# Moving a mixture-of-experts kernel's overflow tiles ahead of its last pair of experts

## The reference: what is computed

```
t = modulate(rms_norm(x))                        # 512 tokens
g = top-1 of 4 groups;  e = top-2 of its 8 experts
hid = silu(t @ w1[e]) * (t @ w3[e])              # 1024 -> 256
out = sum over the two experts of weight * (hid @ w2[e])
x = x + gate * out
```

## Time and profile before

| | us |
|---|---|
| median of 3 runs | 1247.36 (1244.38 to 1254.65) |
| the profiled execution's own time | 1244.05 |
| its span, first to last instruction | 1242.2 |
| PE busy | 1071.7 (86%) |
| DVE busy | 620.3 (50%) |
| ACT busy | 330.4 (27%) |
| POOL busy | 94.2 (8%) |
| q1, SP's transfers | 291.39 MB, 57.9% of 16 engines' span |

### The profile page before, as it was taken

How to read it: one execution, slowest core, us unless ns; L and a number is a source line. 1 busy time by engine, 2 the same in 40 slices (tenths; PEclk the granted TensorE clock), 3 DMA queues, 4 the chain that set the end, 5 groups by cost and what they waited for, 6 DMA issues and landing times.

```text
span 1242.2 us, 15651 instructions
## 1 busy us (share of the span) xinstructions
PE 1071.7 (86%) x5804; PEld 653.8 (53%) x5804; DVE 620.3 (50%) x1500; ACT 330.4 (27%) x913; POOL 94.2 (8%) x121
## 2 busy tenths in 40 slices
PE   2799999898999999877769899898998899877775
PEld 2344444555458666544436555554458666544442
DVE  6999699786337222221146477775237222212133
ACT  3411111675220211111124455564111211111010
POOL 1000000000000011101100000000000111111111
PEclk9999999998998999999999999999998999999998
DMA  9877777207725899999977200103325899999981
GB/s 376 330 287 313 304 301 288 85 2 297 295 96 215 344 420 419 419 420 419 416 276 294 114 1 35 68 1 161 128 86 236 326 420 421 419 420 418 420 361 73
DMA packets 63042, 333.03 MB, mean 268 GB/s; under 512 B 10543, under 2 KB 10799, under 8 KB 31600
## 3 DMA queue, kind: packets, MB, share of 16 engines
q1 hardware_dynamic: 46928, 291.39, 57.9%
q0 software_dynamic: 13824, 33.37, 7.0%
q10 hardware_dynamic: 2208, 7.18, 1.5%
HBM read 316.67 MB, written 32.52 MB: 281 GB/s over the span
## 4 chain that ended last, share of the span: by engine, by line
PE 50%; DMA 23%; DVE 17%; issue 4%; ACT 4%; SPq 1%; DVEq 0%; ACTq 0%; POOLq 0%
PE PP L622 9%; PE PP L695 8%; DMA RQK<-in_moe_w 8%; DMA AHS<-in_moe_w 8%; PE PP L710 5%; DMA ring<-in_moe_w 5%; PE PP L513 4%; DVE AHS L1251 3%; PE PP L785 3%; PE PP L537 3%; PE PP L827 2%; DVE ring L1251 2%; PE PP L831 2%; PE PP L574 2%; PE PP L585 2%
## 5 line engine op out<-in xcount | busy, mean ns | idle before, releaser
L513 PE MATMUL PP<-ring,AHS 128*128 128x512 f32 x384 | 169.2, 597 | 7.2 <-DMA ring<-in_da_w_qkv 7.2
L1572 DVE TENSOR_TENSOR PS<-PS,PP 128x256 f32<-128x256 f32 x33 | 13.9, 421 | 230.6 <-PE PP L695 230.6
L513 PEld LDWEIGHTS PP<-ring,AHS 128*128 128x128 f32 x384 | 72.3, 192 | 92.1 <-issue 92.1
L622 PE MATMUL PP<-ring,AHS 128*128 128x512 f32 x256 | 113.2, 601 | 0.8 <-ACT AHS L1122 0.8
L1582 DVE SCALAR_TENSOR_TENSOR PS<-PP,small,GF 128x512 f32<-128x512 f32 x66 | 46.5, 746 | 118.8 <-PE PP L710 118.8
L695 PE MATMUL PP<-RQK,RV 128*64 128x256 f32 x768 | 86.8, 381 | 20.6 <-issue 17.0
L695 PE MATMUL PP<-ring,RV 128*64 128x256 f32 (+1 forms) x672 | 79.2, 380 | 11.5 <-issue 11.5
L695 PEld LDWEIGHTS PP<-RQK,RV 128*64 128x64 f32 x768 | 64.7, 137 | 45.7 <-issue 30.7
L695 PE MATMUL PP<-AHS,RV 128*64 128x256 f32 x640 | 72.5, 380 | 11.2 <-issue 11.2
L622 PEld LDWEIGHTS PP<-ring,AHS 128*128 128x128 f32 x256 | 49.0, 194 | 60.0 <-issue 60.0
L695 PEld LDWEIGHTS PP<-ring,RV 128*64 128x64 f32 (+1 forms) x672 | 60.4, 140 | 33.8 <-issue 20.5
(11 more groups left out here) (302 smaller groups left out, 1598.9 us busy)
## 6 DMA issues: line engine op xcount, KB each, us to landing
RQK<-in_moe_w SPq DMA_DIRECT2D x72, 1024.0 KB
ring<-in_moe_w SPq DMA_DIRECT2D x63, 1024.0 KB, 22.2
AHS<-in_moe_w SPq DMA_DIRECT2D x60, 1024.0 KB, 28.3
ring<-in_ada_t SPq DMA_DIRECT2D x24, 1024.0 KB, 22.2
AHS<-in_ada_t SPq DMA_DIRECT2D x24, 1024.0 KB, 18.6
ring<-in_da_w_qkv SPq DMA_DIRECT2D x12, 1024.0 KB, 7.0
y_d<-GF POOLq DMA_DIRECT2D x2, 4096.0 KB, 31.0
AHS<-y_d ACTq DMA_DIRECT2D x6, 1024.0 KB, 11.5
```

The source lines that it names most:

```text
L513: last = mm(PB[n % 4][:, :], HT[:, c, t * P:(t + 1) * P], us[c // 4][:, (c % 4) * NH:(c % 4 + 1) * NH], start=c == 0, stop=c == C - 1)
L622: last = mm(PB[2 * t + n][:, :], (OT, OTM)[l][:, k, t * P:(t + 1) * P], us[k // 2][:, (k % 2) * D + n * NH:(k % 2) * D + (n + 1) * NH], st ...
```

## The change

Pairs 0 to 14 run as before. Then come the branches and the overflow tiles, and then pair 15 (`BETWEEN = LAST`). An overflow tile's rows are scattered to `y_d` by POOL, so its 0/1 matrix, its four mixes and its adds go away. All overflow tiles now use the ring bank, and their loads stand on SP's queue ahead of pair 15's. The steps of a tile no longer share the pairs' semaphores but have their own (`oturn`, `omod`, `oab`, `osil`, `ohid`, `ohT`, `oy`, `oyD`), and within a tile w1 and w3 are one group of matmuls with one signal. The pairs' semaphores (`a`, `b`, `sil`, `hid`, `ht`, `hT`, `y`, `xA`, `xD`, `xgt`, `yD`) count on from layer 0 to layer 1. `load_rows` also waits for POOL's `rows`. The turn of tile 16's rows between the products of pair 15 is gone; an overflow tile turns its own. In layer 1 each token tile's mix of pair 15 is added and then at once its sum. The diff, cut to its core:

```diff
+BETWEEN = LAST
@@ sync
-                for n in range(PAIRS):
+                for n in range(BETWEEN):
                     experts(l, n)
                 sp.wait_ge(sem("ctl"), l + 1)
                 tails = sp.value_load(CTL[0:1, 0:1], min_val=0, max_val=TAILS)
                 def overflow(i, b):
...
+                        if isinstance(i, int):
+                            sp.wait_ge(sem(pair_done), PAIRS * l + BETWEEN - 1)
+                        else:
+                            sp.wait_ge(sem(f"{tile_done}{l}"), j - 1)
+                        sp.dma_start(stored(l, RING_BANK)(2 * m + b),
...
                 overflow_steps(sp, tails, overflow)
+                for n in range(BETWEEN, PAIRS):
+                    experts(l, n)
@@ tensor
+            def overflow_tile(l, i, b):
+                j, tiles = 2 * i + b, ((0, OVER, b),)
+                w = stored(l, RING_BANK)
+                pe.wait_ge(sem(f"gath{l}0"), 16 * (PAIRS // 2 + 1 + j))
+                turn_rows(0, sem(f"oturn{l}"))
+                pe.wait_ge(sem(f"wt{l}{b}"), 48 * i + 48)
+                pe.wait_ge(sem(f"omod{l}"), 2 * j + 2)
+                into_hidden(PB[2], 0, w, 0, tiles)
+                into_hidden(PB[3], 0, w, 1, tiles).then_inc(sem(f"oab{l}"), 1)
+                pe.wait_ge(sem(f"ohid{l}"), j + 1)
+                turn_hidden(sem(f"oturn{l}"))
+                pe.wait_ge(sem(f"ohT{l}"), j + 1)
+                out_of_hidden(w, tiles).then_inc(sem(f"oy{l}"), 1)
+                pe.wait_ge(sem(f"oyD{l}"), j + 1)
 
             def experts(l):
+                turn_pair(l, 0)
+                for n in range(BETWEEN):
+                    expert_step(l, n)
+                pe.wait_ge(sem("xA"), PAIRS * l + BETWEEN + 1)
+                pe.wait_ge(sem("xD"), PAIRS * l + BETWEEN + 1)
+                pe.wait_ge(sem("yD"), PAIRS * l + BETWEEN)
+                pe.wait_ge(sem(f"gath{l}0"), 16 * (PAIRS // 2 + 1))
                 pe.wait_ge(sem("ctl"), l + 1)
                 tails = pe.value_load(CTL[0:1, 0:1], min_val=0, max_val=TAILS)
                 def overflow(i, b):
...
+                    overflow_tile(l, i, b)
                 overflow_steps(pe, tails, overflow)
+                for n in range(BETWEEN, PAIRS):
+                    expert_step(l, n)
+                for t in range(T if l else 0):
+                    mix_last(1, t)
@@ scalar, load_rows
+                act.wait_ge(sem("rows"), l + 1)
@@ scalar, between the overflow tiles and pair 15
+                fn(sd[:, 7:8], eps, ACT.Silu)
@@ vector
+                for t in range(T if l else 0):
+                    add_last(1, t)
+                    add_sums(t).then_inc(sem("res"), 1)
@@ gpsimd, after pairs 0 to 14
+                def overflow(i, b):
...
+                    if b or not isinstance(i, int):
+                        pool.wait_ge(sem(f"oturn{l}"), 2 * j - 1)
+                        gather(0, token_at)
+                    pool.wait_ge(sem(f"oyD{l}"), j + 1)
+                    scatter(0, row_at)
+                    pool.wait_ge(sem(f"scat{l}0"), 16 * (half + 1 + j))
+                overflow_steps(pool, tails, overflow)
+                pool.sem_inc(sem("rows"), 1)
```

More of the change, by code:

```diff
@@ L671, in route, with turn_rows @@
                 keep_busy(3, 20)
[L673 to L677 removed]
+            def turn_rows(b, done):
                 for c in range(C):
                     last = nc.tensor.transpose(PB[c % 2][:, (c // 2) * P:(c // 2 + 1) * P], xg[b][:, c * P:(c + 1) * P], ident[:, :])
[L680 to L700 removed]
@@ new lines, in turn_rows, with turn_pair, into_hidden @@
+                last.then_inc(done, 1)
+            def turn_pair(l, n):
+                b, m = n % 2, PAIRS * l + n
+                pe.wait_ge(sem(f"gath{l}{b}"), 16 * (n // 2 + 1))
+                wait(pe, sem("xA"), m)
+                wait(pe, sem("xD"), m)
+                turn_rows(b, sem("xgt"))
+            def into_hidden(o, b, w, m, tiles):
+                for c in range(C):
+                    for s0, s1, e in tiles:
+                        last = mm(o[s0:s1, 0:FF], xgT[b][:, c, s0:s1], w(2 * m + e)[:, c * FF:(c + 1) * FF],
+                                  start=c == 0, stop=c == C - 1)
+                return last
@@ L701, in expert_step, with turn_hidden, out_of_hidden @@
+            def turn_hidden(done):
                 for c in range(2):
                     last = nc.tensor.transpose(PB[4][:, c * P:(c + 1) * P], hid[:, c, :], ident[:, :])
-                last.then_inc(sem(f"ht{l}"), 1)
-                arrived(2)
-                pe.wait_ge(sem(f"hT{l}"), n + 1)
-                wait(pe, sem(f"yD{l}"), n)
+                last.then_inc(done, 1)
+            def out_of_hidden(w, tiles):
                 for m in range(2):
@@ L710, in expert_step, with arrived @@
                             last = mm(PB[5 + m][s0:s1, :], hidT[:, c, s0:s1],
-                                      units(4 + e)[:, c * D + m * NH:c * D + (m + 1) * NH], start=c == 0, stop=c == 1)
-                last.then_inc(sem(f"y{l}"), 1)
+                                      w(4 + e)[:, c * D + m * NH:c * D + (m + 1) * NH], start=c == 0, stop=c == 1)
+                return last
+            def expert_step(l, n):
+                tiles = ((0, CAP, 0), (CAP, 2 * CAP, 1))
+                b, m, w = n % 2, PAIRS * l + n, stored(l, n)
+                def arrived(k):
+                    for e in range(2):
+                        slot, value = arrival[l][("moe", n, 2 * k + e)]
+                        pe.wait_ge(s_w[slot], value)
+                arrived(0)
+                pe.wait_ge(sem("xA"), m + 1)
+                pe.wait_ge(sem("xD"), m + 1)
+                wait(pe, sem("sil"), m)
+                into_hidden(PB[2], b, w, 0, tiles).then_inc(sem("a"), 1)
+                arrived(1)
+                wait(pe, sem("hid"), m)
+                into_hidden(PB[3], b, w, 1, tiles).then_inc(sem("b"), 1)
+                if n < LAST:
+                    turn_pair(l, n + 1)
+                pe.wait_ge(sem("hid"), m + 1)
+                wait(pe, sem("hT"), m)
+                turn_hidden(sem("ht"))
+                arrived(2)
+                pe.wait_ge(sem("hT"), m + 1)
+                wait(pe, sem("yD"), m)
+                out_of_hidden(w, tiles).then_inc(sem("y"), 1)
+            def overflow_tile(l, i, b):
[12 more added lines that the diff above has]
+                pe.wait_ge(sem(f"oyD{l}"), j + 1)
             def mix(hot, b, t, banks):
@@ L1153, in gate, with modulate_rows @@
                 fn(v, v, ACT.Exp).then_inc(sem("ele"), 1)
-            def modulate_rows(l, b, n, before):
-                act.wait_ge(sem(f"xt{l}"), n + 1)
-                wait(act, sem(f"b{l}"), before)
+            def modulate_rows(l, b, done):
                 for c in range(0, C, 2):
@@ L1556, in gate, with modulate_rows @@
                 v.tensor_copy(CTL[:, :], tailf[0:1, :]).then_inc(sem("ctl"), 1)
-            def modulate_rows(l, b, n, before):
-                dve.wait_ge(sem(f"xt{l}"), n + 1)
-                wait(dve, sem(f"b{l}"), before)
+            def modulate_rows(l, b, done):
                 for c in range(1, C, 2):
@@ L1892, in layer, with gather @@
                        allow_small_or_imprecise_dtypes=True).then_inc(sem("iota"), 1)
[L1894 to L1904 removed]
+                def gather(b, at):
                     settle()
```

261 lines of the change are left out of this document (118 added, 143 removed).

## The result

| | before | after |
|---|---|---|
| median of 20 runs each | 1246.49 (1240.26 to 1254.65) | 1254.47 (1250.82 to 1261.51) |
| ratio, with its 95% interval | | 1.0068 (1.005 to 1.0087) |
| the profiled execution's own time | 1244.05 | 1252.87 |
| its span | 1242.2 | 1251.1 |
| mean granted clock | 0.982 | 0.974 |

The forecast was 1252.5 us, worked out on the profiled execution (which took 1252.87), and "within 1%"; both hold, and the loss is clear of the noise.

What follows compares the result with a forecast made beforehand. Serial chains were taken to bound it: layer 1's end on PE and DVE, and layer 0's pair 15 through the `y_d` loads to the next weights. Layer 0 +8.6 and layer 1 +0.1, +8.7 on 1244.05, gave 1252.5 us; range 1241 to 1262.

Steps and rivals of the forecast that it cites:

- Layer 0, the jump: PE's branch over all tiles, now ahead of pair 15, stalls 6.45 us, with +0.1 to the first matmul.
- the turn's -0.3: Layer 0, pair 15: tile 16's turn leaves it while DVE's product still stands there, saving 0.3 us.
- All of it passed on by the chain: Layer 0: pair 15's delay, +7.1 us, goes in full through the `y_d` loads to the next layer's first weights.
- jumps in what is fetched are free: Rival, both layers: PE's jumps land in instructions already fetched and cost nothing, giving 1241 us; chance 0.17.
- Layer 0, the clock: Layer 0, behind the jump: PE's matmuls run slow after standing 8.8 us, +1.5 us, between 0 and 3.7.
- The rival of the full queues: Both layers: the jump's fetch waits behind streaming weights on the same DMA engines, giving 1264 us; chance 0.15.
- its extra 6.45: Layer 0: weights in flight hold the jump as much again, so that it costs 12.9 us.
- Layer 1, up to pair 15's start: Layer 1, pair 14's rows to pair 15: load, turn, modulation, products, clock +1.7 and jump +3.4 us, ending at 1209.0.
- Tile's weights: Layer 1: the tile's last load lands between 1189.4 and 1196.5, needed at 1189.8; taken as 0, bound 6.7 us.
- The end: Layer 1, adds and sums behind pair 15: done at 1237.3 against 1237.16 before, +0.1 us; outputs stay 5.0 us behind.
- bound by POOL's sum rather than by DVE: Sign expected at layer 1's end: the last add waits for POOL's sum of 2.48 us behind the fourth `y_d` load.
- up to 1 less: Layer 1's outputs: 5.0 us behind the last sum, possibly less by up to 1 us because they come spaced out.

Runs made afterwards that it cites:

- e2: The kernel before with PE's two loop copies of an overflow tile left out of its program; ratio to before 0.999 (0.9965 to 1.0015).
- e1: The changed kernel with PE's two loop copies of an overflow tile left out of its program; ratio to before 0.9984 (0.9961 to 1.0008).
- e3: The changed kernel with PE's waits for pair 14's rows, turned rows and gather moved from ahead of the count's load into the tile's code; ratio to before 0.9992.
- e5: The changed kernel with one tile copy in line and one in the loop on every engine, plus e3's moved waits; ratio to before 0.9966.
- e10: The changed kernel with 36 dummy matmuls (144 instructions) at PE's start, shifting all later PE code; ratio to before 1.0033.
- e9: e5 with dummy matmuls in the tile's gaps (14 and 7) and without PE's wait for the tile's rows at its end; ratio to before 0.9937.
- e6: e3 with 36 dummy matmuls on PE in layer 0 ahead of the load of the count; ratio to before 1.0029.

## Why the prediction was right, step by step

The prediction's sum has a slip: 1244.05 + 8.7 is 1252.75, not 1252.5. Its "+0.4%" sets that against the median of before, which is 3.3 us above the execution it adds to; like for like the sum is +0.7%, and 0.68% was measured.

The numbers are those of the profiled executions, from the start of pair 14's w2 product. The difference of the spans, 8.9 us, is made of: 2.3 less upstream (1.7 of it a product of pair 13 that ran at the low clock in before's execution, the rest not traced; I take it for chance, as e2's execution, in the old order, has that start at 616.21), 7.5 from pair 14 of layer 0 to the mla projection (41.66 less 34.14), 1.5 from there to pair 14 of layer 1, and 2.1 from there to the end (63.3 against 61.2).

How the loss divides over the stages is less sure than the total, for before's execution is only one. e2 has the old order, short jumps and the time of before (0.999), yet from pair 14's w2 product to the mla projection it took 37.15 us and not 34.14:

```profile
653.36 7.61 PE L788 MATMUL PP<-ring,AHS 128*128 128x384 f32 x16 [6.10 <-DMA ring<-in_mla_w_in]
```

Against e2 the changed kernel loses 4.5 us in that stretch, gains 1.1 in the next and loses 2.9 at the end; with 0.6 upstream that makes the 6.9 by which the spans differ. Before starts pair 14's w2 product 2.9 us later than e2, and both reach the mla projection at the same time (653.23 and 653.36). So read the stage figures below, which are against before, as good to 2 or 3 us.

- **Layer 0, the jump: right.** Predicted 7.4 us to pair 15's start (the turn's -0.3 lies behind it), measured 7.44. The jump was 5.93 (taken 6.45), the load of the count and what lies around it 0.5 more than taken. e1 shows that 5.6 of it is the jump, e3 that the waits ahead of it uncover it. How much of it arrives is less sure: pair 15's w2 product comes 7.1 us later than in before (23.48 against 16.40) and 5.6 later than in e2 (17.88), where pair 15's second product stood 2.05 us for its weights and ran at half rate. "All of it passed on by the chain" holds against before's execution, not against e2's. That jumps in what is fetched are free was right as a mechanism (e1, e5, e10's layer 1) and wrong for this kernel, as its chance of 0.17 said.
- **Layer 0, the clock: right in size, not in its account.** Predicted +1.5. Pair 15's two products lost 2.1 us by it (9.48 against 7.34), but I had missed a saving: before, the second product waited 1.24 us for its weights (the gap that the profile calls "issue"; with the delay the weights are there, and the 64 run in one). The mla projection's first 16 matmuls took 6.79 us for 5.40, which is most of the 1.5 behind it; but in e2 they took 7.61, so this isn't the change's doing. The sum of layer 0 and the stretch to layer 1 is 9.0, predicted 8.6; against e2 it is 3.4. That the two agree so well is in part luck.
- **The rival of the full queues did not come.** The jump took 5.93 us with weights in flight, no longer than 6.45. Layer 0's is longer than layer 1's in every kernel that has both (5.93, 6.09, 6.25, 4.93, 5.15 against 3.33, 3.63, 3.73, 3.87, 3.68), and the q8 packet shows where: it begins 3.4 us behind the branch in layer 0 and 1.0 in layer 1, while the packet itself (1.1 and 0.9 us) and the rest behind it (1.4) are alike. What holds it back was not tried; only the transfers in flight differ that I know of (281 GB/s at 624 to 626 us, 13 at 1213 to 1217), so the rival's mechanism may be part of the 5.93 though its extra 6.45 did not come.
- **Layer 1, up to pair 15's start: right within 1.2.** Turn at +6.2 (predicted 6.2), jump 3.33 (3.4), steps between the same. The clock took 2.4 on turn and products (0.9 and 1.5) where I had 1.7; the other 0.5 is spread over the steps, which end at 29.18 for 28.0.
- **Tile's weights: right at 0.** They land 7.4 us behind the w2 product's start (e3), needed at 9.9.
- **The end: the term that was mis-sized.** I took 10.0 us for four adds and four sums and let POOL's sums bound them at 0.8 more. The `y_d` loads were early enough (the last 12.4 us behind the first issue, the quiet end of my bounds of 12.3 to 16.5), and DVE bound the end, against the sign that was given ("bound by POOL's sum rather than by DVE"); its sums slowed to 2.06 us beside POOL's: 12.1 us. The outputs gave back 0.9 (4.06 for 5.0), the "up to 1 less". So layer 1 is +2.1 where I had +0.1: 1.2 up to pair 15, 0.5 within it (the clock), 1.3 in the adds and sums, less 0.9 at the outputs.
- **The sum** came within 0.2 of the measured 8.9 by luck: the 2.3 us upstream went against the 2.0 of layer 1 and the 0.4 of layer 0. The medians differ by 8.0.

## What to carry to other kernels

Before a branch is moved, look in the old profile for what its jump is hidden under, and count the instructions that it skips on the engine with the longest code: on PE the eight skips of about 100 to 230 instructions here cost 0.4 us at most wherever they stood, those of 320 to 800 cost 3.3 to 6.5 us where they stood badly. Put waits behind such a branch, not ahead of it, so that it runs under matmuls already queued. And cost a gap on PE with the matmuls behind it, which often ran at the low clock: 0.9 to 2.1 us here. Not every gap did it: in the changed kernel pair 14's second product ran at full rate (3.67 us) behind 2.30 us of idle, and before's mix behind 3.79.

## What the runs showed that I had not expected

- The profiler records the fetch of instructions: one 16 KB packet on q8 stands under every long branch and under no short one. Look there before a "gap for issue" is blamed on anything else.
- A stall can sit one instruction behind a branch that looks free (e10: 0.47 us, then 4.17), and 144 idle instructions at the program's start decide where the fetch is paid 600 us later.
- f32 adds on DVE with both inputs in SBUF and on POOL slow each other, 1.23 to 2.06 and 2.36 to 3.2 us, while DVE's adds with one input in PSUM (L1453, 1.27 for two) do not. The Trainium skill's "SBUF — State Buffer", section "SBUF: two separate sides", describes it as an exclusive lock for just such operations; these rows fit that and don't tell a lock from sharing.
- Dummy matmuls held the clock in e9, where little opened behind them, and not in e6: e9's left 0.5 us at most and all that followed ran at full rate, e6's left 2.5 us and the clock fell to 0.57 of full.
